# Banded attention of a fused transformer block: pairs of heads, a fused mask and maximum, normalisation on GpSimd

## What is computed

```
q = apply_rope(qkv[..., :Q_DIM]) * scale            # 16 heads of 64
k, v = apply_rope(...), ...                         # 4 key/value heads, shared by 4 query heads each
kz, vz = keys and values of the 256 context tokens
s_win = where(|query - key| <= 128, q @ k.T, -1e30)
s_ctx = q @ kz.T
s_sink = sink[head]                                 # one extra logit per head, without a value
p = softmax(concatenate([s_win, s_ctx, s_sink]))
o = p[..., window] @ v + p[..., context] @ vz
yx = o @ w_o
```

## Time and profile before

| what | value |
|---|---|
| median of three runs | 3087.32 us (3086.01 to 3090.15) |
| the profiled execution: its time, its span | 3090.11 us, 3088.3 us |
| TensorE busy | 2896.0 us, 94% |
| VectorE, ScalarE, GpSimd busy | 62%, 49%, 25% |
| mean granted TensorE clock | 0.962 of 2.4 GHz |
| attention, from the first mask (L1722) to the output projection's first matmul | 1511.9 to 1619.75 us |
| TensorE idle just before its first score (L763) | 11.9 us |

### The profile page before, as it was taken

The page is one execution under the profiler, slowest core; times in us unless marked ns, Lnnn a source line. Parts: engine busy times, 40 slices in busy tenths (PEclk is TensorE's granted clock), DMA queues, the critical chain, the costliest instruction groups (busy, mean ns, idle before and its releaser), DMA issues.

```text
span 3088.3 us, 59780 instructions
## 1 busy us (share of the span) xinstructions
PE 2896.0 (94%) x23682; PEld 2727.8 (88%) x23682; DVE 1910.9 (62%) x2539; ACT 1506.8 (49%) x2021; POOL 773.5 (25%) x721
## 2 busy tenths in 40 slices
PE   6999999999999999999788999998689999985999
PEld 5999999999999999999547998997389999973899
DVE  4646647776475564764575546657856566578664
ACT  3434434444344443544355646647256465572663
POOL 1313302223042240330012312308013123160230
PEclk9999999999999999999899999999699999986999
DMA  8775666656666566665003554553035555530454
GB/s 299 246 271 200 220 217 233 204 205 232 232 204 233 203 228 211 225 236 197 25 1 122 184 192 135 195 185 129 14 116 184 192 169 192 185 104 14 138 185 154
DMA packets 152571, 548.95 MB, mean 178 GB/s; under 512 B 16784, under 2 KB 20672, under 8 KB 152000
## 3 DMA queue, kind: packets, MB, share of 16 engines
q1 hardware_dynamic: 148496, 537.99, 51.4%
q10 hardware_dynamic: 3888, 8.30, 0.7%
HBM read 544.38 MB, written 1.84 MB: 177 GB/s over the span
## 4 chain that ended last, share of the span: by engine, by line
PE 86%; DVE 7%; issue 3%; ACT 2%; ACTq 1%; POOL 1%; DMA 0%; SPq 0%; DVEq 0%; POOLq 0%
PE ps L400 26%; PE ps L402 26%; PE ps L401 25%; PE ps L427 2%; PE ps L784 1%; PE ps L763 1%; PE ps L693 1%; ACT sq L1048 1%; ACT w_hi L372 1%; PE ps L863 1%; DVE w_lo L380 0%; DMA modraw<-wmod 0%; DVE AT L1905 0%; PE ps L772 0%; POOL sq L2060 0%
## 5 line engine op out<-in xcount | busy, mean ns | idle before, releaser
L380 DVE TENSOR_TENSOR w_lo<-raw,w_hi 128x1024 fp32r<-128x1024 f32 x880 | 1143.6, 1315 | 719.4 <-ACT w_hi L372 717.5
L400 PE MATMUL ps<-h_hi,w_hi 128*128 128x256 f32 x4976 | 1418.2, 285 | 28.7 <-DVE w_lo L380 11.6
L402 PE MATMUL ps<-h_hi,w_lo 128*128 128x256 f32 x4976 | 1407.9, 283 | 0.0
L401 PE MATMUL ps<-h_lo,w_hi 128*128 128x256 f32 x4976 | 1403.5, 282 | 0.0
L372 ACT ACTIVATE w_hi<-raw 128x1024 fp32r<-128x1024 f32 x880 | 905.2, 1054 | 498.3 <-PE ps L402 496.8
L400 PEld LDWEIGHTS ps<-h_hi,w_hi 128*128 128x128 f32 x4976 | 939.7, 189 | 43.7 <-issue 28.4
L402 PEld LDWEIGHTS ps<-h_hi,w_lo 128*128 128x128 f32 x4976 | 959.6, 193 | 0.0
L401 PEld LDWEIGHTS ps<-h_lo,w_hi 128*128 128x128 f32 x4976 | 941.6, 189 | 1.5 <-issue 0.5
L2064 POOL CAST u_hi<-ut 128x256 fp32r<-128x256 f32 (+1 forms) x258 | 239.8, 929 | 1495.9 <-DVE ut L1611 788.1
L400 PE MATMUL ps<-u_hi,w_hi 128*128 128x256 f32 (+1 forms) x2064 | 589.3, 286 | 0.0
L401 PE MATMUL ps<-u_lo,w_hi 128*128 128x256 f32 (+1 forms) x2064 | 581.3, 282 | 0.0
(11 more groups left out here) (292 smaller groups left out, 1995.0 us busy)
## 6 DMA issues: line engine op xcount, KB each, us to landing
raw<-wst SPq DMA_DIRECT2D x880, 512.0 KB, 3.5
modraw<-wmod SPq DMA_DIRECT2D x132, 512.0 KB, 5.4
headraw<-wmod SPq DMA_DIRECT2D x12, 512.0 KB, 10.1
mtab<-mixtabs ACTq DMA_DIRECT2D x2, 1280.0 KB, 6.2
xT<-xin ACTq DMA_DIRECT2D x2, 1024.0 KB, 23.4
atab<-attabs ACTq DMA_DIRECT2D x1, 1024.0 KB, 6.1
out<-xT SPq DMA_DIRECT2D x1, 1024.0 KB, 4.8
skew<-sqb ACTq DMA_DIRECT2D x1, 768.0 KB, 3.3
```

The costliest lines, as they stand in the source:

```text
L380: dve.tensor_tensor(w_lo[:, s, :], raw[:, s, :], w_hi[:, s, :], ALU.subtract).then_inc(S("lo_ready"), 1)
L400: pe.matmul(psum, wh, hi, start=start, stop=False)
L401: pe.matmul(psum, wh, lo, start=False, stop=False)
L402: return pe.matmul(psum, wl, hi, start=False, stop=stop)
```

## The change

- **Order of the splits and ropes.** `lo_upto` leaves `first_qkv_dve` and runs behind the five ropes. A small exponential on `spare` is put ahead of ScalarE's copies for the context.
- **Pairs.** The stage goes over 16 pairs p (both heads of a pair, one query block). Both scores of a pair are issued behind each other into two banks; `scores(p+2)` now comes after `turn(p)`.
- **Mask and maximum** become one VectorE instruction, `tensor_tensor_reduce`: (scores + mask) x -1 is written, and its minimum with the negated sink goes to `top_w`. The exponential takes scale -1.
- **Sinks.** Both sink terms of a pair are made with one subtraction and one exponential.
- **Normalisation** moves to GpSimd, between the splits of the outputs.
- **Turned probabilities:** ScalarE copies the first head's out of PSUM, VectorE the second's.
- **Values:** for each of the four key tiles, first head and second head in turn; once in two pairs.
- `sw`, `pw` and `pn` get four slots; sums and maxima have columns of their own.

(Indentation shortened by 12 columns where there is that much.)

```diff
@@ -46,7 +46,7 @@
 N_IN = 25
 KTAPS = 31
 PER_CHUNK = 3
-SCORE_BANK = (0, 1, 6, 7)
+PAIRS = 16
 LEVELS = 6
 POOL_X = 2
@@ -317,11 +317,14 @@
 atab = sb("atab", [P, attabs.shape[1]], F32, c1)
 rp1 = sb("rp1", [P, 2, 2, T], F32, c1)
 rp2 = sb("rp2", [P, 2, 2, T], F32, c1)
-sw = sb("sw", [P, 2, 2 * T], F32, c1)
-pw = sb("pw", [P, 2, 2 * T], F32, c1)
-pn = sb("pn", [P, 2, 2 * T], F32, c1)
-PTw = sb("PTw", [P, 2, 4, T], F32, c1)
-aw = sb("aw", [P, 2, 8], F32, c1)
+sw = sb("sw", [P, 4, 2 * T], F32, c1)
+pw = sb("pw", [P, 4, 2 * T], F32, c1)
+PTw = sb("PTw", [P, 2, 2, 4, 2 * P], F32, c1)
+pn = sb("pn", [P, 4, 2 * T], F32, c1)
+top_w = sb("top_w", [P, DC, 4], F32, c1)
+sum_w = sb("sum_w", [P, DC, 4], F32, c1)
+sink_w = sb("sink_w", [P, DC, 4], F32, c1)
+nsink = sb("nsink", [P, 2 * DC], F32, c1)
         with ExitStack() as c1:
 Z = sb("Z", [P, N_IN, T], F32, c1)
 mtab = sb("mtab", [P, mixtabs.shape[1]], F32, c1)
@@ -681,7 +684,7 @@
     for m in range(10):
         src = AK[:, m, 0:T] if m < 2 else AQ[:, m - 2, :]
         mm = pe.matmul(ps[:, 2 + m // 2, T * (m % 2):T * (m % 2 + 1)], permW, src, start=True, stop=True)
-    mm.then_inc(S("w_perm"), 1)
+    mm.then_inc(S("w_turned"), 1)
     for n in range(8, 12):
         if n >= 10:
             pe.wait_ge(S("w_evac"), n + 3)
@@ -751,50 +754,58 @@
     for n in range(2):
         for t in range(4):
             mm = pe.transpose(ps[:, (7, 1)[n], P * t:P * (t + 1)], AV[:, n, P * t:P * (t + 1)], ident)
-    mm.then_inc(S("w_vt"), 1)
+    mm.then_inc(S("w_turned"), 1)
     pe.wait_ge(S("w_rope"), 5)
-    pe.wait_ge(S("w_vv"), 2)
-    def scores(n):
-        cc, hf, qb = n // 4, n // 2 % 2, n % 2
-        r = slice(64 * hf, 64 * hf + 64)
-        if n >= 4:
-            pe.wait_ge(S("w_sb"), n - 3)
-        pe.matmul(ps[:, SCORE_BANK[n % 4], 0:512], AQ[r, cc, P * qb:P * (qb + 1)], AK[r, cc // 4, :],
-                  start=True, stop=True).then_inc(S("w_s"), 1)
-    def turn(n):
-        pe.wait_ge(S("w_pn"), n + 1)
-        if n >= 2:
-            pe.wait_ge(S("w_pt"), n - 1)
+    def scores(p):
+        cc, qb = p // 2, p % 2
+        if p >= 2:
+            pe.wait_ge(S("w_sb"), 2 * (p - 1))
+        elif p == 1:
+            pe.wait_ge(S("w_vv"), 2)
+        for hf in range(2):
+            r = slice(64 * hf, 64 * hf + 64)
+            mm = pe.matmul(ps[:, 2 - 2 * qb + hf, 0:512], AQ[r, cc, P * qb:P * (qb + 1)], AK[r, cc // 4, :],
+                           start=True, stop=True)
+        mm.then_inc(S("w_s"), 1)
+    def turn(p):
+        for hf in range(2):
+            pe.wait_ge(S("w_pn"), 2 * p + hf + 1)
+            if p >= 1:
+                pe.wait_ge(S("w_pt_dve" if hf else "w_pt_act"), p)
+            for t in range(4):
+                mm = pe.transpose(ps[:, 4 + hf, P * t:P * (t + 1)], pn[:, 2 * (p % 2) + hf, P * t:P * (t + 1)],
+                                  ident)
+            mm.then_inc(S("w_tr"), 1)
+    def values(cc):
+        if cc == 0:
+            pe.wait_ge(S("w_vv"), 2)
+        else:
+            pe.wait_ge(S("gated"), c["hid"] + max(cc - 1, 0))
+        pe.wait_ge(S("w_pt_act"), 2 * cc + 2)
+        pe.wait_ge(S("w_pt_dve"), 2 * cc + 2)
         for t in range(4):
-            mm = pe.transpose(ps[:, 2 + n % 2, P * t:P * (t + 1)], pn[:, n % 2, P * t:P * (t + 1)], ident)
-        mm.then_inc(S("w_tr"), 1)
-    def values(n):
-        cc, hf = n // 4, n // 2 % 2
-        pe.wait_ge(S("w_pt"), n + 1)
-        if hf == 0 and cc >= 2:
-            pe.wait_ge(S("gated"), c["hid"] + cc - 1)
-        r = slice(64 * hf, 64 * hf + 64)
-        for t in range(4):
-            v0 = P * (cc // 4) + 64 * hf
-            mm = pe.matmul(ps[r, 4 + cc % 2, 0:T], VV[:, t, v0:v0 + 64], PTw[:, hf, t, :],
-                           start=(t == 0), stop=(t == 3))
+            for hf in range(2):
+                r = slice(64 * hf, 64 * hf + 64)
+                v0 = P * (cc // 4) + 64 * hf
+                mm = pe.matmul(ps[r, 6 + cc % 2, 0:T], VV[:, t, v0:v0 + 64], PTw[:, cc % 2, hf, t, :],
+                               start=(t == 0), stop=(t == 3))
         mm.then_inc(S("w_pv"), 1)
     scores(0)
     scores(1)
-    for n in range(32):
-        if n + 2 < 32:
-            scores(n + 2)
-        turn(n)
-        if n % 2 == 0 and n:
-            values(n - 1)
-    values(31)
+    for p in range(PAIRS + 1):
+        if p < PAIRS:
+            turn(p)
+        if p + 2 < PAIRS:
+            scores(p + 2)
+        if p >= 2 and p % 2 == 0:
+            values((p - 2) // 2)
 def pair_slot(h):
@@ -1208,6 +1219,7 @@
             position_act(c, n // 2)
         for step in QKV_ACT.get(n, ()):
             chain_act(c["chain"], step)
+    act.activation(spare[:, 0:1], epsc[:, 0:1], ACT.Exp)
     for n in range(8, 12):
         act.wait_ge(S("unit_done"), d + n + 1)
         dst = AK[:, n - 8, T:2 * T] if n < 10 else AV[:, n - 10, T:2 * T]
@@ -1245,33 +1257,38 @@
     root(c, N, 1.0 / D)
 def attn_act(c):
-    act.wait_ge(S("w_vt"), 1)
+    act.wait_ge(S("w_turned"), 2)
     for n in range(2):
         act.activation(VV[:, :, P * n:P * (n + 1)],
                        ps[:, (7, 1)[n], :].rearrange("p (t v) -> p t v", t=4), ACT.Copy).then_inc(S("w_vv"), 1)
-    def pt(n):
-        hf, qb = n // 2 % 2, n % 2
-        act.wait_ge(S("w_tr"), n + 1)
-        if n >= 4:
-            act.wait_ge(S("w_pv"), n // 2 - 1)
-        act.activation(PTw[:, hf, :, P * qb:P * (qb + 1)],
-                       ps[:, 2 + n % 2, :].rearrange("p (t q) -> p t q", t=4), ACT.Copy).then_inc(S("w_pt"), 1)
-    for n in range(32):
-        head = 2 * (n // 4) + n // 2 % 2
-        sk = VEC["sink"] + head
-        act.wait_ge(S("w_nm"), n + 1)
-        if n >= 2:
-            act.wait_ge(S("w_pn"), n - 1)
-        act.activation(pw[:, n % 2, :], sw[:, n % 2, :], ACT.Exp, bias=aw[:, n % 2, 1:2],
-                       accum_out=aw[:, n % 2, 2:3]).then_inc(S("w_e"), 1)
-        act.activation(aw[:, n % 2, 3:4], vec[:, sk:sk + 1], ACT.Exp,
-                       bias=aw[:, n % 2, 1:2]).then_inc(S("w_e"), 1)
-        if n >= 1:
-            pt(n - 1)
-    pt(31)
+    def exponentials(p, hf):
+        act.wait_ge(S("w_sb"), 2 * p + hf + 1)
+        if p >= 2:
+            act.wait_ge(S("w_pn"), 2 * (p - 2) + hf + 1)
+        n = 2 * (p % 2) + hf
+        at = 2 * (p % 2) + hf
+        act.activation(pw[:, n, :], sw[:, n, :], ACT.Exp, scale=-1.0, bias=top_w[:, p // 2, at:at + 1],
+                       accum_out=sum_w[:, p // 2, at:at + 1]).then_inc(S("w_e"), 1)
+    def turned(p):
+        act.wait_ge(S("w_tr"), 2 * p + 1)
+        if p >= 4:
+            act.wait_ge(S("w_pv"), p // 2 - 1)
+        act.activation(PTw[:, p // 2 % 2, 0, :, P * (p % 2):P * (p % 2 + 1)], ps[:, 4, :].rearrange("p (t q) -> p t q", t=4),
+                       ACT.Copy).then_inc(S("w_pt_act"), 1)
+    for p in range(PAIRS):
+        exponentials(p, 0)
+        exponentials(p, 1)
+        act.wait_ge(S("w_sk"), p + 1)
+        at = 2 * (p % 2)
+        act.activation(sink_w[:, p // 2, at:at + 2], sink_w[:, p // 2, at:at + 2], ACT.Exp).then_inc(S("w_e"), 1)
+        if p >= 1:
+            turned(p - 1)
+    turned(PAIRS - 1)
 def mix_act(c):
     b, d, l = c["unit"], c["unit"], c["l"]
@@ -1654,7 +1671,6 @@
             position_dve(c, n // 2)
         for step in QKV_DVE.get(n, ()):
             chain_dve(c["chain"], step)
-    lo_upto(dve, d + 14)
 def out_dve(c):
     b, nk = c["unit"], c["nk"]
@@ -1693,60 +1709,77 @@
 def attn_dve(c):
     hid = c["hid"]
-    steps = [0]
-    def own(ins):
-        ins.then_inc(S("w_own"), 1)
-        steps[0] += 1
-        dve.wait_ge(S("w_own"), steps[0])
-    dve.wait_ge(S("w_perm"), 1)
+    dve.wait_ge(S("w_turned"), 1)
     dve.wait_ge(S("atab_loaded"), 32)
     for n in range(5):
         dst = AK[:, :, 0:T] if n == 0 else AQ[:, 2 * n - 2:2 * n, :]
         cs = ropeW[0 if n == 0 else 2].unsqueeze(1).broadcast_to([P, 2, T])
         sn = ropeW[1 if n == 0 else 3].unsqueeze(1).broadcast_to([P, 2, T])
-        dve.tensor_tensor(rp1[:, n % 2], dst, cs, ALU.mult).then_inc(S("w_rp"), 1)
+        dve.tensor_tensor(rp1[:, n % 2], dst, cs, ALU.mult).then_inc(S("w_own"), 1)
         dve.tensor_tensor(rp2[:, n % 2], ps[:, 2 + n, :].rearrange("p (a t) -> p a t", a=2), sn,
-                          ALU.mult).then_inc(S("w_rp"), 1)
-        dve.wait_ge(S("w_rp"), 2 * n + 2)
+                          ALU.mult).then_inc(S("w_own"), 1)
+        dve.wait_ge(S("w_own"), 2 * n + 2)
         dve.tensor_tensor(dst, rp1[:, n % 2], rp2[:, n % 2], ALU.add).then_inc(S("w_rope"), 1)
-    def top(n):
-        qb = n % 2
-        sk = VEC["sink"] + 2 * (n // 4) + n // 2 % 2
-        dve.wait_ge(S("w_s"), n + 1)
-        if n >= 2:
-            dve.wait_ge(S("w_e"), 2 * (n - 1))
-        dve.tensor_tensor(sw[:, n % 2, :], ps[:, SCORE_BANK[n % 4], :], bandW[:, qb, :], ALU.add).then_inc(S("w_sb"), 1)
-        dve.wait_ge(S("w_sb"), n + 1)
```

(80 more changed lines are left out.)

## The result

The changed kernel takes **3092.86 us** (median of 20 runs, 3087.24 to 3095.5), the kernel before on the same chip 3087.84 (20 runs, 3083.76 to 3090.99): a ratio of **1.0015, 95% interval 1.0008 to 1.0022**. So it is slower by 5 us: clear of the noise by the interval, but less than the 0.2% that the prediction took as the least that tells. 13 us faster was forecast, and 3086 was the end of the range.

A forecast was written before the change was run, and what follows sets the result against it. Bound: a ring in which each engine waits its turn, 6.12 us per two half-steps. Start 11.8 us earlier, then rings of 6.71 and a tail, ended the stage at 1606.7 instead of 1619.75: 13 us earlier, 3074.3 us, range 3055 to 3086.

The forecast's parts named there:

- price of a normalisation on GpSimd: One 128x512 TENSOR_SCALAR on GpSimd: 0.93 us, from L2054's 0.551 for 256 columns; bounds 0.62 and 1.456.
- the fixed 0.17: Column-independent part of a GpSimd instruction, some 0.17 us, from TENSOR_TENSOR's 0.728 for 256 columns and 1.287 for 512.
- The start: Before the stage, splits moved behind the ropes: first fused instruction at 1500.1 instead of the mask at 1511.91, 11.8 us earlier.
- The ring: Per pair, mask, reciprocal, normalisations, transposes and scores in series: 5.68 us at full clock, 7.09 at half; 6.12 before.
- Masks, sinks and reciprocal to GpSimd: VectorE's part of the ring: two fused instructions 1.46, then sink, sum, reciprocal and hand-over 0.56; 2.02 us together.
- A fused instruction: VectorE's mask and maximum in one pass, in the ring: 0.73 us each, between 0.60 and 1.45.
- The second head's transposes: Four TensorE transposes in the ring after the second normalisation: 0.66 us at full clock; the first head's are hidden.
- both scores with hand-over: Both heads' scores on TensorE, closing the ring, running side by side: 1.09 us at full clock, the price of one.
- The values: Beside the ring, two heads' products run at once: sixteen take 1.94 us, 3.68 at half clock, adding 0.6 every second pair.
- The clock: TensorE at half clock for six tenths of the stage: ring 6.71 us, stage end 13 us earlier.
- Rival 3: GpSimd's normalisation takes 1.456 us in this stage, clock stays at half, values hidden: 3097 us; chance 0.06.
- The turning point: At half clock, result turns slower when one normalisation exceeds about 1.1 us, measurably slower from 1.35.

The follow-up runs named there:

- e5: Changed kernel with GpSimd's normalisation written as two operations (times the reciprocal, plus a column of zeros): 3065.82 us, ratio 0.9933 to the kernel before.
- e4: Changed kernel with a plain GpSimd copy in place of the normalising multiply (division left out): 3062.48 us, ratio 0.9924 to the kernel before.
- e6: Changed kernel with GpSimd's multiply taking the constant 0.5 instead of the reciprocal column (division left out): 3089.87 us, one run; kernel before 3087.72.
- e1: Changed kernel with both normalisations of a pair on VectorE, behind the reciprocal, instead of GpSimd: 3067.22 us, ratio 0.9942 to the kernel before.
- e7: Changed kernel with scores(p+2) ahead of turn(p) and both normalisations on VectorE: 3030.52 us, ratio 0.9812 to the kernel before.
- e8: Changed kernel with scores(p+2) ahead of turn(p) and GpSimd's normalisation written as two operations: 3028.54 us, ratio 0.9809 to the kernel before.
- e2: Changed kernel with only scores(p+2) issued ahead of turn(p) instead of behind it: 3048.42 us, ratio 0.9875 to the kernel before.

## Why the prediction was wrong

**The step that failed** is the price of a normalisation on GpSimd: "I take 0.93, the same operation". L2054 is the same instruction by its name and not by its form, two operations against one. The form in the kernel took 1.564, and 0.768 with a second operation added (e5); for the form that it belonged to, the scaling to 512 columns was 0.16 too high, because the fixed 0.17 came from another operation. The error, 0.63 us, comes 32 times: 20.2 us. It turns the forecast's 13 us faster into 7 slower; 5.0 was measured.

By stretches the forecast had 8.5 us to pair 2's mask, 87.2 for 13 rings and 10.9 from pair 15's mask to the projection. Measured: 9.86, 101.14, 14.62. With the right price the forecast would have been 9.8, 103.6 and 13.4. The same sum holds for the other prices. With 0.613, 0.768, 1.489 and 1.564 put in for 0.93 it gives 3064, 3069, 3092 and 3095 us; e4, e5, e6 and after took 3062.5, 3065.8, 3089.9 and 3092.9.

- **The start**: 11.8 forecast, 11.9 measured.
- **The ring** as drawn was right, and so were its other terms. Masks, sinks and reciprocal to GpSimd: 2.02 forecast, 1.99 (1558.77 to 1560.76). A fused instruction 0.73, measured 0.67 from start to start. The second head's transposes at full clock 0.66, measured 0.58 to the scores; both scores with hand-over 1.09, measured 1.18. The ring with the normalisation put right: 5.68 + 1.26 = 6.94 at full clock, 6.91 measured; 7.09 + 1.26 = 8.35 at half, 8.33 measured.
- **The values**: two heads at once, as forecast. They did not stand out of the ring by the 0.6 that I had added, because the longer normalisation covered them. In the tail they did. Its rows in the timeline of after:

```profile
1610.95 3.11 POOL L2109 TENSOR_SCALAR pn<-pw,sum_w 128x512 f32<-128x512 f32 x2
...
1612.07 3.68 PE L796 MATMUL ps<-PTw,VV 128*64 128x256 f32 x16
...
1615.69 1.46 PE L780 MATMUL ps<-tabs,pn 128*128 128x128 f32 x8
...
1618.02 1.95 PE L796 MATMUL ps<-PTw,VV 128*64 128x256 f32 x16 [0.87 <-DVE PTw L1753]
```

Sixteen records took 3.68 at half clock and 1.95 at full, as eight did before. GpSimd was done with pair 15 at 1614.06, and its transposes stood behind the values until 1615.69.

- **The clock**: half in six tenths of the stage was forecast, 68.3 of 125.1 us measured. This was the least certain of my numbers, and that it came out near is partly luck: it was meant for a ring of 5.7 to 7.4 us, and the ring was 7.8. In e5, whose ring of 5.94 is inside that, it was 41.0 of 97.1, four tenths.
- **Rival 3** had nearly the right price, with another cause, and 0.06. It gave 3097 for 1.456 us, and what I held against it, "nothing on VectorE that contends", was true and beside the point: 1.564 was measured with nothing contending. The turning point that I gave, 1.1 us, was for a stage wholly at half clock, and is too low for this one: on a line between e5 (0.768, ratio 0.9933) and after (1.564, 1.0015) the ratio is 1 at some 1.4 us (an estimate), and at 1.489 e6's single run is 1.0007. "Measurably slower from 1.35" did not come true either: 1.564 cost 0.15%. The range was too narrow because it left out the high end of the price, 1.456, which I had named as a bound myself.
- **The pages.** The Trainium skill, "GPSIMD Engine Reference", section "4.1 Engine selection", calls one-input operations roughly line-rate. The copy (0.613) fits that and the multiply (1.564) doesn't; the measurement decides. Its advice to use VectorE was right for the instruction, 0.483 for the same work (e1); the kernels with 0.483 there and with 0.768 on GpSimd were equally fast (e1 and e5, e7 and e8). The lock that the Trainium skill describes in "SBUF — State Buffer", section "SBUF: two separate sides", lengthened no normalisation, as the prediction had it: 1558 to 1568 ns throughout. The trace agrees with it right behind the stage: GpSimd's CAST (L2097) at 1620.50 took 1.32 us instead of 0.40, beside a split on VectorE with two inputs in SBUF (L383, 1620.35, 1.22 us). For very small instructions it does not: in e2 VectorE's sink subtraction (128x2, both inputs in SBUF), started some 1.23 us before the end of a normalisation, took 0.36 to 0.38 us instead of 0.16 and did not wait for that end, and there the measurement decides.

What the trace of before could have told: L2036, on the same engine and under the same name as L2054, had one operation like the new instruction, at 0.85 to 1.06 for half the columns, beside a busy VectorE. Its 1.53 for 512 would have given 19 us more than the forecast, 6 slower than before.

Left open: why the one-operation form is slower (only times are shown), and which part of the two-operation form makes it faster.

## What to carry to other kernels

Price an instruction by a row with the same form (operations, operands, types), not by one with the same name, and if two rows of that name disagree, find out why before choosing. In a ring in which every engine waits its turn, ask first what is queued behind the new wait: moving the scores ahead of it gained 43 us here, a cheaper instruction 25 in the old order. Then price the instruction itself, since each of its nanoseconds counts once per turn.
